# The last expert of a mixture-of-experts layer as one packed set of 64 high and 64 low columns

## The reference, cut to what matters

```python
logits = (xt @ router).astype(jnp.float32)
top_logit, top_idx = lax.top_k(logits, TOP_K)          # TOP_K = 2, 8 experts
gates = jax.nn.softmax(top_logit, axis=-1)
...
def _swiglu(h, w1, w3, w2):                            # w1, w3: 1024 x 1408, w2: 1408 x 1024
    return (jax.nn.silu(h @ w1) * (h @ w3)) @ w2
```

## Time and profile before

| | us |
|---|---|
| median of 3 runs | 1939.27 |
| lowest, highest | 1939.12, 1943.13 |
| the profiled execution | 1944.72 |
| its span, first to last instruction | 1942.9 |
| PE busy | 1882.1 (97%) |
| DVE busy | 1310.0 (67%) |
| ACT busy | 943.8 (49%) |

### The profile page before, as it was taken

The page is one execution under the profiler, slowest core; times in us unless marked ns, Lnnn a source line. Parts: engine busy times, 40 slices in busy tenths (PEclk is TensorE's granted clock), DMA queues, the critical chain, the costliest instruction groups (busy, mean ns, idle before and its releaser), DMA issues.

```text
span 1942.9 us, 34150 instructions
## 1 busy us (share of the span) xinstructions
PE 1882.1 (97%) x14477; PEld 1737.7 (89%) x14477; DVE 1310.0 (67%) x1864; ACT 943.8 (49%) x1150; POOL 124.2 (6%) x82
## 2 busy tenths in 40 slices
PE   9999999999999999999999999999999999889998
PEld 9889999999988999998888888888899989789978
DVE  7975566654599647665556668989888456856563
ACT  5353345434444423444435457767756453445453
POOL 0000000000000000000100011010200001100034
PEclk9999999999999999999999999999999999999999
DMA  8221246455542223544545568999945333314320
GB/s 309 88 88 56 100 165 224 163 185 184 182 140 88 72 63 134 197 171 158 182 153 194 182 229 312 331 328 335 334 180 173 131 109 119 111 54 164 131 88 23
DMA packets 52679, 321.84 MB, mean 166 GB/s; under 512 B 6320, under 2 KB 9648, under 8 KB 19760
## 3 DMA queue, kind: packets, MB, share of 16 engines
q1 hardware_dynamic: 52096, 317.76, 46.5%
q10 hardware_dynamic: 432, 1.90, 0.3%
HBM read 317.01 MB, written 1.05 MB: 164 GB/s over the span
## 4 chain that ended last, share of the span: by engine, by line
PE 78%; DVE 14%; ACT 4%; issue 3%; POOL 0%; DVEq 0%; ACTq 0%; POOLq 0%
PE b L383 77%; DVE s_arena L399 5%; DVE s_ring_lo L501 3%; ACT s_wh L408 2%; PE b L2055 1%; DVE s_arena L1433 1%; DVE s_arena L2456 1%; DVE s_arena L402 0%; ACT s_arena L408 0%; ACT s_arena L405 0%; DVE s_arena L637 0%; DVE s_arena L2377 0%; DVE s_roots L399 0%; ACT s_arena L411 0%; POOL s_ring_lo L501 0%
## 5 line engine op out<-in xcount | busy, mean ns | idle before, releaser
L501 DVE TENSOR_TENSOR s_ring_lo<-s_ring,s_wh 128x2048 fp32r<-128x2048 f32 (+3 forms) x310 | 648.1, 2096 | 309.3 <-ACT s_wh L408 308.7
L408 ACT ACTIVATE s_wh<-s_ring 128x2048 fp32r<-128x2048 f32 (+3 forms) x332 | 574.1, 1732 | 253.2 <-PE b L383 249.2
L383 PE MATMUL b<-s_Hh,s_wh 128*128 128x256 f32 x1832 | 536.2, 293 | 9.2 <-DVE s_arena_r L2983 4.2
L383 PE MATMUL b<-s_Hl,s_wh 128*128 128x256 f32 x1832 | 521.6, 285 | 0.0
L383 PE MATMUL b<-s_Hh,s_ring_lo 128*128 128x256 f32 x1832 | 521.4, 285 | 0.0
L383 PEld LDWEIGHTS b<-s_Hh,s_wh 128*128 128x128 f32 x1832 | 354.5, 194 | 20.0 <-issue 10.2
L383 PEld LDWEIGHTS b<-s_Hl,s_wh 128*128 128x128 f32 x1832 | 354.8, 194 | 0.5
L383 PEld LDWEIGHTS b<-s_Hh,s_ring_lo 128*128 128x128 f32 x1832 | 354.4, 193 | 0.0
L383 PE MATMUL b<-s_wh,s_arena_r 128*128 128x512 f32 (+1 forms) x942 | 296.4, 384 | 4.5 <-DVE s_arena_r L2294 3.7
L383 PE MATMUL b<-s_arena_r,s_wh 128*128 128x256 f32 x1184 | 214.6, 282 | 4.7 <-DVE s_arena L399 1.7
L383 PEld LDWEIGHTS b<-s_wh,s_arena_r 128*128 128x128 f32 x942 | 176.0, 188 | 38.9 <-DVE s_arena_r L2294 4.9
(11 more groups left out here) (195 smaller groups left out, 1925.1 us busy)
## 6 DMA issues: line engine op xcount, KB each, us to landing
s_ring<-fixed SPq DMA_DIRECT2D x158, 1024.0 KB, 4.9
s_ring<-experts SPq DMA_DIRECT2D x96, 1024.0 KB, 5.0
s_ring<-experts SPq DMA_DIRECT2D x48, 768.0 KB, 4.4
s_ring<-fixed SPq DMA_DIRECT2D x24, 256.0 KB, 4.1
s_c<-c SPq DMA_DIRECT2D x1, 1664.0 KB, 17.6
s_ring<-fixed SPq DMA_DIRECT2D x3, 512.0 KB, 5.9
s_arena<-s_arena SPq DMA_DIRECT2D x48, 32.0 KB, 1.9
s_c<-c ACTq DMA_DIRECT2D x1, 1344.0 KB, 6.1
```

What stands on the lines that cost most here:

```text
L383: return e.matmul(out, l, r, start=start, stop=True, skip_group_check=True)
L408: return e.activation(out, x, ACT.Copy, scale=scale)
L501: e.tensor_tensor(l_, r_, h_.bitcast(F), SUB).then_inc(*up(engine, z % "lo", i))
```

## The change

The set of turn 7 joins the packed ones. A constant row `turns` takes the place of `iota` where turns are assigned to experts; it is filled from RANKS = (0, ..., 7), so it holds the same numbers. Three places are made general: the ACT copy of a packed unit waits for the packed unit before it (by a list of all packed units), and `gather_dve` skips the low matrix of a group whose tokens are all packed, and puts the event on the packed instruction.

```diff
-    "c0": [("id", 128), ("blk", 128), ("ones", 128), ("iota", 8)],
+    "c0": [("id", 128), ("blk", 128), ("ones", 128), ("iota", 8), ("turns", 8)],
...
+    put("turns", np.tile(np.array(RANKS), (128, 1)) * 1.0)
...
+RANKS = (0, 1, 2, 3, 4, 5, 6, 7)
...
-        PACKED = {(2, 1)}
+        PACKED = ((2, 1), (7, 0))
...
+        packed = [(p, ch, s) for p, ch, s in UNITS if (p, s) in PACKED]
...
-            e.tensor_tensor(m_which, m_q.unsqueeze(1).broadcast_to([128, 8, 8]), c("iota").unsqueeze(2).broadcast_to([128, 8, 8]),
+            e.tensor_tensor(m_which, m_q.unsqueeze(1).broadcast_to([128, 8, 8]), c("turns").unsqueeze(2).broadcast_to([128, 8, 8]),
                             ALU.is_equal).then_inc(*up("V"))
...
                     for q in range(2):
-                        stt(e, m_H[g % 2][0][:, 2 * jj + q, o + 64:o + 128], b[:, T * q + o:T * q + o + 64], pc("nf1", 2 * jj + q),
-                            m_H[g % 2][0][:, 2 * jj + q, o:o + 64].bitcast(F), MUL, SUB).then_inc(*up("V"))
-            for q in range(2):
+                        last = stt(e, m_H[g % 2][0][:, 2 * jj + q, o + 64:o + 128], b[:, T * q + o:T * q + o + 64], pc("nf1", 2 * jj + q),
+                                   m_H[g % 2][0][:, 2 * jj + q, o:o + 64].bitcast(F), MUL, SUB)
+                        last.then_inc(*(up("V", "slot lo", g, jj) if q and not n_ else up("V")))
+            for q in range(2 if n_ else 0):
...
-                                    if ch:
-                                        e.wait_ge(*on("hidden", t - SETS[p]))
+                                    if packed.index((p, ch, s)):
+                                        e.wait_ge(*on("hidden", unit[packed[packed.index((p, ch, s)) - 1]]))
```

## The result

| | before | changed |
|---|---|---|
| median of 5 runs, us | 1939.39 | 1950.43 |
| lowest, highest | 1939.12, 1943.13 | 1947.94, 1950.66 |
| ratio, 95% interval | | 1.0049 (1.0037 to 1.0061) |

What follows compares the result with a forecast made beforehand. PE was taken to lead by little, every other engine close behind, with packing making tanh wait for DVE's add. Delays 4.7, gathers -0.9 and clock 2.5 gave +6.3 us on the median 1939.27: 1945.6, range 1940.8 to 1951.0.

Steps and rivals of the forecast that it cites:

- What is taken away: Up and down pieces: 54 matmuls of 512 columns and 16 of 384 go, 15.0 us of PE.
- Gate 0b: Turn 7: tanh waits for DVE's add behind a rest; next piece's rest 2.6 us later, PE idle some 3.6.
- the walk: Step-by-step timing of turns 7 and 8 against the earlier trace's times, giving +4.7 us, range +4.1 to +6.4.
- Gate 1b: Turn 7: a scatter job waits for DVE's spread behind the gate's join; PE idles about 3 us, 2.8 late.
- Gate 2b: Turn 7's end: first own down piece starts 5.1 us late on PE, after an idle time of 3.9.
- Turn 8: Rests, POOL's rests and last turn job keep the pace; exbc 0's rest 4.9 us late, last scatters 4.5.
- The clock: PE drops to half speed after new idle times; zero to three drops, 0 to +5.1 us, taken as +2.5.
- the rival: Clock drops after each of three stalls, once for 6.5 us: +10.4 us, 1949.7; chance 0.15.
- The gathers: Turn 7's four gathers: 32 matmuls of 64 instead of 128 columns give back 0.9 us, between 0 and 1.8.
- The sum: Whole kernel: 4.7 - 0.9 + 2.5 = +6.3 us, added to the median 1939.27 for 1945.6.
- The faster one: Transfer rate limits, not the chain; gate 0b's add ends by about 1352.2; 1933.9 us; chance 0.05.
- The absorbed one: Chain partly absorbed in gaps, no clock drop, POOL out of the way: around +1, 1940.3 us; chance 0.14.

Runs made afterwards that it cites:

- e5: Changed kernel with a third matmul again in each packed step of the last turn, repeating the high weights (sums wrong, timing only): 1949.29 us, ratio 1.0045.
- e6: Changed kernel with 12, 9, 13 and 11 unread matmuls on constants filling PE's four long idle times: 1948.36 us, ratio 1.0038.
- e2: Changed kernel with the last turn's sums of high and low rows written in place in PSUM instead of SBUF: 1948.16 us, ratio 1.0034.
- e4: Changed kernel with DVE doing the gate's add before the rest of piece i + 2 in the last turn: 1946.73 us, ratio 1.0023.
- e7: Changed kernel with both the last turn's sums in PSUM and the gate's add ahead of the rest: 1941.84 us, ratio 1.0003.

## Why the prediction came out as it did

- **What is taken away.** 15.0 us of PE were forecast to be worth nothing by themselves. The 70 matmuls are gone, and by e5 they are worth some 1.3 us, an estimate. That the busy time fell by 14.7 is a coincidence of two clocks, as shown above.
- **Gate 0b.** Forecast: rest of the next piece 2.6 later, idle time 3.6. Measured: 2.58 and 3.33. That part of the walk was right to a tenth.
- **Gate 1b.** Forecast idle time about 3 at the scatter; measured 2.74, and for the same reason, DVE's spread behind the gate's join:

```profile
1387.58 0.58 PE L385 MATMUL b<-s_arena_r 128*128 128x256 f32 x1 [2.74 <-DVE s_X L2092]
```

- **Gate 2b.** Forecast: first own down piece 5.1 late after an idle time of 3.9. From the rest of gate 0a it is at 58.1 us instead of 50.6, 7.6 late, after 3.54 idle. Of that 1.9 are the two times at half clock, by e6, where it comes 5.7 late. So the walk was right here too, to 0.6:

```profile
1403.08 0.50 PE L385 MATMUL b<-s_wh,s_arena_r 128*128 128x512 f32 x1 [3.54 <-DVE s_ring_lo L503]
```

- **Turn 8: the term that failed.** The rest of exbc 0 was to start 4.9 late; it starts 11.1 late (74.8 us after the rest of gate 0a, 63.7 before). I priced collisions with POOL by the one rest of 2.85 us in the earlier trace rows, 0.6 each, with a total of -0.6 to +1.7, and only for the rests, whose operands don't change. The multiply for the hidden value was taken at turn 2's 0.74 us, where POOL happened to be idle. It moved from one operand in PSUM to none, and the whole remainder of POOL's instruction, 2.5 us, fell on it twice. Only the second time did anyone wait for it: 2.6 us between the first own down piece and the last turn job (table at e2). The forecast had this term at nothing.
- **The clock.** +2.5 was taken, from one drop and half of another. There were three, of 3.4, 3.4 and 10.2 us, and the rival had three too, but they cost 3.4 us (e6) and not the rival's 6.6. That DVE sets the pace in most of that time would explain it; it is argued, not shown. The forecast took the idle times' length as the sign of a drop. The trace of before already spoke against that: the same idle time of 2.44 us that the earlier trace rows shows with the clock full behind it stands a second time, at 582.92, with half clock behind it (lines in the last section).
- **The gathers.** 0.9 us was forecast. From the rest of turn 5's first gate piece to that of turn 7's gate 0a the kernel before takes 104.9 us and the changed one 104.6: 0.3. So the value lay nearer to the lower bound; whether a fixed cost per matmul or the added placing instructions on DVE ate the rest is open.
- **The sum.** For the stretch 4.7 + 2.5 = 7.2 us were forecast and 11.4 measured. The missing 4.2 are 2.6 of POOL, which the sum lacked, 0.9 of clock (3.4 in place of 2.5), and 0.7 that no run pins down. By cause, put together from different executions, the 11.4 are about 3.6 for the order (e4 against e6), 2.6 for the operand, 3.4 for the clock and 1.8 left over, near the 2.0 that e7 keeps. The plain differences of the stretches, 4.8 (e2), 6.0 (e4) and 3.4 (e6), make 14.2 because the first two hold some of the clock's part again.
- **Luck.** The direction was right for the reason given. That 1950.4 still lies in the range is luck in part: its upper end of 1951.0 was set for a dearer clock, and what filled it was a term that the forecast did not have.
- **The rivals.** The faster one fell at its named point, the add of gate 0b ending at 1353.98, not before the rest; ACT waited for no landing in the last turn. The absorbed one, at 1940.3, is far off: the walk's delays came in full.

## What to carry to other kernels

A packing that saves matmuls but adds a step on two other engines is worth what those engines can spare at that place, not what the matmuls cost: in the last turn nothing covers the chain. (In turn 2 a second set stands beside it; that it hides the chain there is read from the program, no run took that packing away.) When an engine's program is written out by hand, put the short step that somebody waits for ahead of the long one that works for later, and check where each new operand lies, not only how long the instruction took elsewhere. Pack the product whose result needs no further step, here the down one, first, though here it gained nothing that the totals show. And when two kernels are compared by one traced execution each, set their time at half clock side by side before giving a difference to an edit; a time between two events next to each other, as in the table at e2, is safer than the whole.

## What the runs showed of the hardware that I had not expected

- A VectorE scalar_tensor_tensor with both large operands in SBUF stood until POOL's instruction was through: 3.27 and 3.20 us instead of 0.74 and 0.60 for the same shapes with one operand in PSUM beside the same POOL instruction, and 0.74 with both in SBUF and POOL idle. It works the other way too: where DVE's rest began first, POOL's took 4.07 us in place of 3.51.
- The clock stayed at half, 1.2 GHz, for 10.2 us, in which PE was busy for 7.07 (fence above); the idle times in and around it were 3.54 and 3.13 us.
- The length of PE's idle time alone did not tell whether the clock fell. In the changed kernel it fell after 3.33 and 2.74 us, in e2 it stayed full after 3.31 and 2.71 at the same places, and in e7 it fell to 0.55 from 1386.0 to 1389.4 after 1.91 but not after 2.20 at 1355.30. In one and the same execution of before, 2.44 us of idle time in front of the same line of the program were followed by full clock at 71.85 and by half at 582.92:

```profile
582.92 0.36 PE L1223 MATMUL b<-s_c,s_arena 128*128 128x128 f32 x1 [2.44 <-DVE s_arena L1423]
...
583.00:586.50 3.50, 3.50 (x18) 3.50 (x19) 3.50 (x7) 0.60 (x1) 0.00 (x0) 0.51 0.00 0
```

- A float32 matmul of 128 columns on constants takes 0.23 us and is listed as two.
